# Experts' stationary operands at a pitch of 136 columns in place of 128

## The reference

```
def moe_swiglu(x, router, w1, w3, w2):
    logits = (xt @ router).astype(F32)
    top_v, top_i = lax.top_k(logits, TOP_K)              # 2 of 8
    gates = jax.nn.softmax(top_v, axis=-1)
    ...
    for e in range(N_EXPERTS):
        h = jax.nn.silu(xt @ w1[e]) * (xt @ w3[e])       # 1024 -> 2816
        y = y + dense_gate[:, e:e + 1].astype(x.dtype) * (h @ w2[e])   # 2816 -> 1024
```

## Time and profile before

| what | value |
|---|---|
| median of 3 runs | 1288.58 us (1286.91 to 1292.07) |
| span of the profiled execution | 1288.5 us |
| PE busy | 1247.9 us (97%) |
| DVE busy | 1052.9 us (82%) |
| ACT busy | 837.0 us (65%) |
| stretch of the experts | about 522 to 1273 us of the span |
| TensorE's granted clock | 0.996 over the span |

### The profile page before, as it was taken

One profiled execution on the slowest core, in us unless ns is written; L12 is line 12 of the kernel. 1 busy time (PEld: TensorE's weight loads), 2 busy tenths in 40 slices (PEclk: granted clock), 3 DMA queues, 4 the chain that ended last, 5 costly groups with the idle time before them and its releaser, 6 DMA issues.

```text
span 1288.5 us, 17344 instructions
## 1 busy us (share of the span) xinstructions
PE 1247.9 (97%) x5932; PEld 1034.4 (80%) x5932; DVE 1052.9 (82%) x1049; ACT 837.0 (65%) x863; POOL 126.5 (10%) x111
## 2 busy tenths in 40 slices
PE   7999999999999979999999999999999999999995
PEld 6889877888878857778888888888888888888884
DVE  5778885455567988889899889888998998898996
ACT  4565654444524474578777777777777777787772
POOL 1063001000004912200000000000000000000001
PEclk9999999999999999999999999999999999999998
DMA  9653058666436515899999999999999999999991
GB/s 351 221 183 104 14 191 294 196 190 210 141 129 209 174 49 197 298 382 384 389 380 387 389 380 387 389 380 387 389 381 382 389 380 381 388 369 376 390 370 53
DMA packets 195058, 374.76 MB, mean 291 GB/s; under 512 B 9392, under 2 KB 27952, under 8 KB 194880
## 3 DMA queue, kind: packets, MB, share of 16 engines
q1 hardware_dynamic: 189072, 351.37, 76.8%
q0 software_dynamic: 5936, 22.74, 4.8%
HBM read 363.07 MB, written 11.01 MB: 290 GB/s over the span
## 4 chain that ended last, share of the span: by engine, by line
PE 90%; DVE 5%; DMA 2%; ACT 1%; issue 1%; POOL 0%; SPq 0%; DVEq 0%; ACTq 0%
PE psum L390 22%; PE psum L392 22%; PE psum L391 22%; PE psum L411 4%; PE psum L412 4%; PE psum L413 4%; PE psum L2040 1%; DMA raw<-in_od_w 1%; DVE wlo L381 1%; PE psum L1572 1%; PE psum L1571 1%; PE psum L1570 1%; PE psum L1712 1%; PE psum L1594 1%; PE psum L1596 1%
## 5 line engine op out<-in xcount | busy, mean ns | idle before, releaser
L381 DVE TENSOR_TENSOR wlo<-raw,whi 128x1536 fp32r<-128x1536 f32 (+1 forms) x426 | 676.6, 1622 | 137.9 <-ACT whi L375 136.8
L375 ACT CAST whi<-raw 128x1536 fp32r<-128x1536 f32 (+1 forms) x426 | 581.8, 1376 | 212.6 <-PE psum L392 176.2
L390 PE MATMUL psum<-whi,xe_hi 128*128 128x512 f32 x704 | 277.8, 395 | 2.8 <-DVE wlo L381 2.5
L392 PE MATMUL psum<-whi,xe_lo 128*128 128x512 f32 x704 | 274.6, 390 | 0.0
L391 PE MATMUL psum<-wlo,xe_hi 128*128 128x512 f32 x704 | 274.1, 389 | 0.0
L390 PEld LDWEIGHTS psum<-whi,xe_hi 128*128 128x128 f32 x704 | 132.2, 188 | 31.2 <-DVE wlo L381 4.2
L392 PEld LDWEIGHTS psum<-whi,xe_lo 128*128 128x128 f32 x704 | 132.1, 188 | 28.1
L391 PEld LDWEIGHTS psum<-wlo,xe_hi 128*128 128x128 f32 x704 | 132.3, 188 | 26.5
L390 PE MATMUL psum<-whi,hTe_hi 128*128 128x512 f32 x352 | 138.4, 393 | 0.0
L392 PE MATMUL psum<-whi,hTe_lo 128*128 128x512 f32 x352 | 137.2, 390 | 0.0
L391 PE MATMUL psum<-wlo,hTe_hi 128*128 128x512 f32 x352 | 137.1, 389 | 0.0
(11 more groups left out here) (333 smaller groups left out, 1482.5 us busy)
## 6 DMA issues: line engine op xcount, KB each, us to landing
raw<-in_od_w SPq DMA_DIRECT2D x262, 768.0 KB, 9.8
raw<-in_od_w SPq DMA_DIRECT2D x95, 512.0 KB, 9.4
raw<-in_ev_w SPq DMA_DIRECT2D x33, 768.0 KB, 4.4
raw<-in_ev_w_in SPq DMA_DIRECT2D x32, 512.0 KB, 6.6
raw<-in_od_w_in SPq DMA_DIRECT2D x24, 512.0 KB, 4.6
raw<-in_od_w SPq DMA_DIRECT2D x32, 384.0 KB, 8.0
raw<-in_ev_w SPq DMA_DIRECT2D x12, 512.0 KB, 3.8
raw<-in_od_w SPq DMA_DIRECT2D x24, 256.0 KB, 7.6
```

What stands on the lines that cost most here:

```text
L375: nc.scalar.copy((whi if into is None else into)[i % GT][:, 0:n], src[:, 0:n]).then_inc(hi_done, 1)
L381: nc.vector.tensor_tensor((wlo if into is None else into)[i % GT][:, 0:n], src[:, 0:n], (whi if high is None else high)[i % GT][:, 0:n].bi ...
L390: nc.tensor.matmul(ps, hi, w_h[:, r, :], start=start, stop=False)
L392: ins = nc.tensor.matmul(ps, lo, w_h[:, r, :], start=False, stop=stop)
```

## The change

The four tiles get 136 columns a chunk in place of 128, 8 of them unused. The writers address four chunks of 128 columns with a step of 136 in place of one run of 512; the readers take the first 128 columns of a chunk. No instruction is added, taken away or put elsewhere in the order of its engine, and none changes its waits. The tiles behind the widened ones move up: counted from the weights' remainder, chunk k of `xe_hi` begins at 32k bytes, of `xe_lo` at 256 + 32k, of `hTe_hi` at 32k, of `hTe_lo` at 192 + 32k (all modulo 512), `h_e` stays at 0, and `silu_e`, `pick`, `put`, `y_hi` and `y_lo` stand at 384.

```diff
+PITCH = P + 8
...
-        xe_hi, m3 = at("xe_hi", [P, KD, P], F32R, m2)
-        xe_lo, m4 = at("xe_lo", [P, KD, P], F32R, m3)
+        xe_hi, m3 = at("xe_hi", [P, KD, PITCH], F32R, m2)
+        xe_lo, m4 = at("xe_lo", [P, KD, PITCH], F32R, m3)
         h_e, m5 = at("h_e", [P, FF], F32, m4)
-        hTe_hi, m6 = at("hTe_hi", [P, KF, P], F32R, m5)
-        hTe_lo, m7 = at("hTe_lo", [P, KF, P], F32R, m6)
+        hTe_hi, m6 = at("hTe_hi", [P, KF, PITCH], F32R, m5)
+        hTe_lo, m7 = at("hTe_lo", [P, KF, PITCH], F32R, m6)
...
+        def seated(tile, k0, kc):
+
+            return tile[:, k0:k0 + kc, 0:P]
+
+        def seated_bank(bank, kc):
+
+            return psum[:, bank, 0:kc * P].rearrange("p (k s) -> p k s", s=P)
...
-                    nc.scalar.copy(xe_hi[:, 4 * b:4 * b + 4, :].rearrange("p k s -> p (k s)"), psum[:, 4 + b, :]).then_inc(m_ga_hi, 1)
+                    nc.scalar.copy(seated(xe_hi, 4 * b, 4), seated_bank(4 + b, 4)).then_inc(m_ga_hi, 1)
...
-                nc.vector.tensor_tensor(hTe_lo[:, k0:k0 + kc, :].rearrange("p k s -> p (k s)"), psum[:, bank, 0:kc * P],
-                                        hTe_hi[:, k0:k0 + kc, :].rearrange("p k s -> p (k s)").bitcast(F32),
+                nc.vector.tensor_tensor(seated(hTe_lo, k0, kc), seated_bank(bank, kc), seated(hTe_hi, k0, kc).bitcast(F32),
                                         ALU.subtract).then_inc(m_tlo, 1)
...
-                return [[(psum[:, bank, :], xe_hi[:, k, :], xe_lo[:, k, :], k == 0, k == KD - 1)] for k in range(k0, k0 + kc)]
+                return [[(psum[:, bank, :], xe_hi[:, k, 0:P], xe_lo[:, k, 0:P], k == 0, k == KD - 1)] for k in range(k0, k0 + kc)]
```

More of the change, by code:

```diff
@@ L929, in turn_hi @@
                 act.wait_ge(m_tp, 6 * n + g + 1)
-                nc.scalar.copy(hTe_hi[:, k0:k0 + kc, :].rearrange("p k s -> p (k s)"), psum[:, bank, 0:kc * P]).then_inc(m_thi, 1)
+                nc.scalar.copy(seated(hTe_hi, k0, kc), seated_bank(bank, kc)).then_inc(m_thi, 1)
             def high_parts(n, tiles, last, again):
@@ L1404, in gather_lo @@
                     dve.wait_ge(m_ga_hi, 2 * n + b + 1)
-                    dst = slice(4 * b, 4 * b + 4)
-                    nc.vector.tensor_tensor(xe_lo[:, dst, :].rearrange("p k s -> p (k s)"), psum[:, 4 + b, :],
-                                            xe_hi[:, dst, :].rearrange("p k s -> p (k s)").bitcast(F32),
+                    nc.vector.tensor_tensor(seated(xe_lo, 4 * b, 4), seated_bank(4 + b, 4), seated(xe_hi, 4 * b, 4).bitcast(F32),
                                             ALU.subtract).then_inc(m_ga_lo, 1)
@@ L2055, in up_rows @@
                 bank = 2 * (i // 6 % 2) + (i // 3 % 2 if i < UP_END[-2] else 0)
-                return [[(psum[:, bank, :], xe_hi[:, k, :], xe_lo[:, k, :], k == 0, k == KD - 1)] for k in range(k0, k0 + kc)]
+                return [[(psum[:, bank, :], xe_hi[:, k, 0:P], xe_lo[:, k, 0:P], k == 0, k == KD - 1)] for k in range(k0, k0 + kc)]
             def down_rows(i):
-                return [[(psum[:, 2 * half, :], hTe_hi[:, k, :], hTe_lo[:, k, :], k == 0, k == KF - 1)] for half, k in DN_ROWS[i - N_UP]]
+                return [[(psum[:, 2 * half, :], hTe_hi[:, k, 0:P], hTe_lo[:, k, 0:P], k == 0, k == KF - 1)] for half, k in DN_ROWS[i - N_UP]]
             def block_e(n, b):
```

## The result

The changed kernel takes 1304.2 us (median of 4 runs, 1301.12 to 1305.68) against 1288.64 us (4 runs, 1286.91 to 1292.07): slower by a factor of 1.0118, 95% interval 1.0096 to 1.0139. The forecast was 1303 us.

What follows compares the result with a forecast made beforehand. TensorE was taken as the bound, through the experts' fp32r matmuls; 2912 x 5.0 ns = +14.6 us on the 1288.5 us span, all else 0, gave 1303 us, with a range of 1279 to 1320 us.

Steps and rivals of the forecast that it cites:

- The bound: Experts go at TensorE's pace alone, 93.3 us each; 1 ns per matmul is worth 3.2 us over 8 experts.
- The writers, the moved tiles and the transposes at 0: Stepped copies on ScalarE and VectorE, tiles moved to 384 bytes, and transposes of h_e were each to cost 0.
- The price of 5.0 ns: Each of 2912 fp32r expert matmuls with a shifted chunk was to cost +5.0 ns, +14.6 us in all.
- The reason for the price: Remainders changing between loads leave TensorE's two SBUF streams no stretch to settle at 226.7 ns; slower given 0.48.
- The unsettled matmuls behind the transposes: First fp32r matmuls after four transposes, 232 ns apart on average, 5.3 ns more than later; source of the price.
- The count of 2912: Expert matmuls whose chunk's remainder differs from the weights': 364 of 396 per expert, 2912 in all.
- the chunks that the prediction wanted to see: Chunks 0 of xe_hi and 0 and 16 of hTe_hi, to tell whether the remainder itself or its changing costs.
- Rival A: The remainder has no effect on the expert matmuls, 226.7 ns throughout, 1288.6 us; chance 0.30 together with Rival C.
- Rival B: Equal remainders collide in SBUF, so shifted ones speed the expert matmuls, to 1260 us at the most; chance 0.22.
- Rival C: Stepped writers slow the copies, so xe_lo comes late for an expert's first matmuls; 5 us, 1293 us; chance within Rival A's 0.30.

Runs made afterwards that it cites:

- run 3: Changed kernel with hTe_hi and hTe_lo woven into one tile, writers stepped, every hTe chunk at one remainder; xe keeps 136 columns: 1297.95 us.
- run 10: Kernel before with a pitch of 192 columns in xe_hi alone, chunks at 0 and 256 bytes in turn: 1288.6 us.
- run 1: Kernel before, pitch 128, with all xe chunks 32 bytes and all hTe chunks 256 bytes past the weights' remainder: 1300.2 us.
- run 2: Kernel before, pitch 128, with all xe chunks 64 bytes and all hTe chunks 128 bytes past the weights' remainder: 1306.3 us.
- run 5: Kernel before with all xe chunks 16 bytes and all hTe chunks 96 bytes past the weights' remainder: 1303.6 us.
- run 6: Kernel before with all xe chunks 160 bytes and all hTe chunks 192 bytes past the weights' remainder: 1303.05 us.
- run 7: Kernel before with all xe chunks 224 bytes and all hTe chunks 384 bytes past the weights' remainder: 1304.96 us.
- run 8: Kernel before with xe_hi at 0 and xe_lo at 256 bytes, hTe_hi at 0 and hTe_lo at 128: 1293.5 us.
- run 11: Kernel before with a pitch of 160 columns in xe_hi and xe_lo, chunks at 0, 128, 256 and 384 bytes in turn: 1295.2 us.
- Run 9: Kernel before with whi, wlo and the experts' chunks moved up 32 bytes together, the first layer's xT at distance 224 modulo 256: 1296.4 us.

## Why the prediction was right, and where not

**The bound.** Right. TensorE set the pace before and after, and 1 ns of a matmul's spacing was worth nearly what was said. The 396 matmuls of an expert grew by 1.93 us, 4.9 ns each, or 15.4 us for all eight experts at that rate; they grew by 14.5, since the sum left out that TensorE waits in the first one.

**The writers, the moved tiles and the transposes at 0.** Right: the copies took the same time, run 3 and run 10 have stepped writers with the experts at 226.7 ns, and in the changed kernel the transposes of `h_e` still take 0.44 us for four, as before.

**The price of 5.0 ns.** The size was right. Over 2912 matmuls the 14.5 us are 5.0 ns each, and 1.93 us over the 364 of one expert are 5.3. The profiled spans differ by 15.4 us against 14.6 forecast, 0.8 of it ahead of the experts. The prediction also took the span for the time of a run; in every run that has both, the time is 1.7 to 1.8 us above the span (1305.68 and 1303.9 for the changed kernel). That the span of the kernel before lay 0.1 us from its median was chance, and the difference between the kernels does not hang on it.

**The reason for the price.** Wrong in part. The prediction said that "the remainder changes with every third matmul and again between the high part and the rest, so the pattern that gives 226.7 ns has no stretch in which to settle". Runs 1, 2, 5, 6 and 7 have nothing that changes, and settle, but at 233 ns or so for all distances but 16 (in part), 192 and 256. `xe` in runs 8 and 10 has a remainder that changes all the time and stays at 226.7 ns. What stands in its place: the distance between the chunk that is loaded and the weights that stream decides the spacing, and 0 and 256 bytes are free. The changed kernel walks through all eight multiples of 32 modulo 256. Their mean in the table (0, 32, 64, 96, 128, 160, 192, 224) is 231.9 ns; the changed kernel has 232.3 and 233.1. So it lies 0.4 and 1.2 ns above that average. The average is not a rule: in runs 8 and 11 it was 2.6 and 2.0 ns too low. The unsettled matmuls behind the transposes, from which the 5 ns were read, gave nearly the same number. They may run through many relative positions of the two streams too, in time and not by address, but nothing shows that this is why the numbers agree. As far as the runs show, the right size came from a wrong reason, and by luck.

**Which chunks are free.** The count of 2912 took the remainders modulo 512, so that `xe_lo`'s first chunk at 256 and some of `hTe` counted as costly. Modulo 256 it is 11 x (2 x 7 + 7) + 2 x (2 x 19 + 19) = 345 of 396, 2760 in all. Runs 8 and 11 show that even this count is loose, since a costly load slows a neighbour at a free distance too. The changed kernel shows it as well, at the chunks that the prediction wanted to see: over its trace the matmuls beside which a chunk at distance 0 modulo 256 is loaded take 229.3 ns on `xe` and 234.0 on `hTe`, and not 226.7.

**Rival A, no effect.** Out. Run 9 settles it: the same instructions change their spacing when only the distance does. The Trainium skill's "SBUF — State Buffer", section "SBUF: two separate sides", has the weight load and the moving operand on two ports that are independent. The trace does not agree for fp32r, if independent means that neither slows the other: 226.7 against 233.3 ns by where the one begins against the other. Where in the chip the two meet, no run shows.

**Rival B, faster.** Out. None of the eleven distances tried was better than equal remainders, and none went below 226.7. The Trainium skill's "TensorE: Matmul & The Clock Gate", section "Back-to-back issue gap", gives N / 2.4 + 2.5 ns for an isolated matmul at full clock, 215.8 for 512 columns. No distance reached it.

**Rival C, the writers.** Out, by run 3 and by the durations of the copies.

## What to carry to other kernels

When TensorE is busy all the time, read the distance from start to start, or the page's mean in nanoseconds, and not the timeline's duration: the 5 ns that this change cost are lost in its hundredths of a microsecond. With fp32r operands of the shapes used here, let every stationary chunk begin at the same remainder modulo 256 bytes as the moving rows; a pad between the chunks cost 1.2% here, and chunks offset as a whole cost up to 1.4% (1306.3 us in run 2 against 1287.9). If a pitch must be wider, 64 columns more (256 bytes) were free in `xe_hi` where 8 and 32 were not in `xe`.

## What the runs showed of the hardware that was not expected

- The settled spacings of a 512-column fp32r matmul were mostly one of two: 226.7 ns, which is 13.3 more than 512 columns at 2.4 GHz, and 233.3 ns, which is 20.0 more. At 16 bytes both occurred in the same kernel, each for a whole block of matmuls.
- The price seems to go by the distance modulo 256: 0 and 256 agree (226.7 both), 128 and 384 nearly (232.4, and 233.3 or 232.3 by the stretch), and no other pair was tried. It is not even: 192 cost 2.2 ns and 64 cost 6.6.
- A single costly load among free ones slowed the matmul beside which it was loaded and the one after it (232.4 and 233.8 ns in run 8).
- Not settled: what the two streams collide on, why the first matmuls behind transposes are slower at distance 0, what picks the pattern at 16 bytes, whether a full-fp32 or a 2-byte product has the same rule, and whether a distance between those tried lies below 226.7 ns.
